# Where the norm of the differential heads is computed: ahead of the output projection, or among the products of its first two strips

## The reference

```python
def odd_mixer(h, w_qkv, w_out, lam_q1, lam_k1, lam_q2, lam_k2, subln, layer):
    ...
    y = differential_attention(q, k, v, lam)        # 8 heads, 1024 tokens, 128 features each
    y = rmsnorm(y, subln, SUBLN_EPS) * (1.0 - lam_init)   # over the 128 features of one head
    y = y.transpose(0, 2, 1, 3).reshape(B, T, N_HEADS_C * 2 * HEAD_DIM)
    return y.astype(h.dtype) @ w_out

def differential_attention(q, k, v, lam):
    ...
        p = jax.nn.softmax(s, axis=-1)
        a = p[:, :, 0] - lam * p[:, :, 1]
        return jnp.einsum('bhqk,bhkd->bhqd', a, v)
```

## Time and profile before

| | |
|---|---|
| median of 3 runs | 2777.64 us (2775.39 to 2777.65) |
| profiled execution, its own time | 2779.66 us |
| its span, first to last instruction | 2777.9 us |
| PE busy | 2682.9 us, 97% |
| DVE, ACT busy | 1773.7 us, 64%; 1114.9 us, 40% |
| chain that ended last | PE 87%, DVE 4%, ACT 4%, issue 3% |

### The profile page before, as it was taken

One profiled execution on the slowest core, in us unless ns is written; L12 is line 12 of the kernel. 1 busy time (PEld: TensorE's weight loads), 2 busy tenths in 40 slices (PEclk: granted clock), 3 DMA queues, 4 the chain that ended last, 5 costly groups with the idle time before them and its releaser, 6 DMA issues.

```text
span 2777.9 us, 37690 instructions
## 1 busy us (share of the span) xinstructions
PE 2682.9 (97%) x13632; PEld 2185.7 (79%) x13632; DVE 1773.7 (64%) x2905; ACT 1114.9 (40%) x1986; POOL 139.9 (5%) x142
## 2 busy tenths in 40 slices
PE   8999999879999999999999999999899999999998
PEld 6787777668788888888777778888787888888886
DVE  4555655554666666666667777776456667666665
ACT  4555545433432223223445445545234222322333
POOL 0000022310000000000010000000000000000001
PEclk9999999979999999999999999999999999999999
DMA  3122233441111111111211111112211111111112
GB/s 118 52 57 80 53 96 110 135 113 61 42 50 57 54 45 53 49 57 46 95 63 45 45 48 51 46 45 69 80 57 42 57 54 46 53 49 57 46 50 76
DMA packets 106220, 173.73 MB, mean 63 GB/s; under 512 B 33376, under 2 KB 42976, under 8 KB 104032
## 3 DMA queue, kind: packets, MB, share of 16 engines
q1 hardware_dynamic: 95136, 162.28, 19.1%
q10 hardware_dynamic: 10944, 9.57, 1.3%
HBM read 151.74 MB, written 20.08 MB: 62 GB/s over the span
## 4 chain that ended last, share of the span: by engine, by line
PE 87%; DVE 4%; ACT 4%; issue 3%; DMA 1%; POOL 1%; SPq 1%; ACTq 0%; POOLq 0%; DVEq 0%
PE PS L1877 18%; PE PS L1879 18%; PE PS L1878 18%; PE PS L1958 15%; PE PS L2091 4%; PE PS L2030 4%; PE PS L2053 3%; ACT EC L849 1%; PE PS L2068 1%; PE PS L2046 1%; PE PS L2015 1%; PE PS L1971 1%; PE PS L2072 1%; DVE HL L1565 1%; PE PS L1884 1%
## 5 line engine op out<-in xcount | busy, mean ns | idle before, releaser
L1958 PE MATMUL PS<-HH,WS 128*128 128x512 f32 x1536 | 527.7, 406 | 14.9 <-DVE WS L1278 11.4
L1958 PEld LDWEIGHTS PS<-HH,WS 128*128 128x128 f32 x1536 | 289.8, 190 | 74.0 <-DVE WS L1278 11.4
L1077 ACT ACTIVATE WS<-WR 128x512 fp32r<-128x512 f32 x254 | 159.3, 629 | 459.8 <-PE PS L1879 318.6
L1958 PE MATMUL PS<-HL,WS 128*128 128x512 f32 x768 | 304.0, 396 | 0.0
L1676 DVE TENSOR_TENSOR X<-PS,X 128x512 f32<-128x512 f32 x352 | 232.7, 685 | 80.6 <-PE PS L1879 78.6
L1877 PE MATMUL PS<-AH,WS 128*128 128x512 f32 x704 | 280.2, 398 | 3.1 <-issue 1.8
L1879 PE MATMUL PS<-AH,WS 128*128 128x512 f32 x704 | 278.9, 396 | 0.0
L1878 PE MATMUL PS<-AL,WS 128*128 128x512 f32 x704 | 278.5, 396 | 0.0
L1877 PE MATMUL PS<-TH,WS 128*128 128x512 f32 x640 | 251.6, 393 | 1.1 <-DVE WS L1618 1.1
L1879 PE MATMUL PS<-TH,WS 128*128 128x512 f32 x640 | 249.9, 391 | 0.0
L1878 PE MATMUL PS<-TL,WS 128*128 128x512 f32 x640 | 248.8, 389 | 0.0
(11 more groups left out here) (221 smaller groups left out, 4656.0 us busy)
## 6 DMA issues: line engine op xcount, KB each, us to landing
WR<-wstrips SPq DMA_DIRECT2D x304, 256.0 KB, 2.7
DR<-wdown SPq DMA_DIRECT2D x88, 256.0 KB, 2.6
X<-x SPq DMA_DIRECT2D x8, 1024.0 KB, 8.2
BIASC<-ali_c SPq DMA_DIRECT2D x8, 960.0 KB, 6.9
Y<-y_scratch SPq DMA_DIRECT2D x14, 512.0 KB, 8.5
BIAS<-tab_b SPq DMA_DIRECT2D x4, 1536.0 KB, 8.1
BIAS<-ali_a SPq DMA_DIRECT2D x4, 1152.0 KB, 7.9
ya_scratch<-YS ACTq DMA_DIRECT2D x32, 128.0 KB, 2.4
```

What stands on the lines that cost most here:

```text
L1077: e.activation(WS[:, slot, 0, :], src, ACT.Copy).then_inc(S["w_hi"], 1)
L1958: last = e.matmul(ps, wt, xt, start=g == 0, stop=g == 23)
```

## The change

The tiles EC0 and EC1 get two buffers each, taken in turn by blocks, and the wait before the exponential is loosened by one block. In the last pair the squares of the heads come earlier (`SQUARED_AT`), and the second strip's weights are rounded at n = 3. The mean of heads 0 to 6 stands in DVE's list at n = 6; root, reciprocal and a new way of spreading stand ahead of `hi(15, 7)` and `lo(15, 7)`: PE turns RT into rows (64 rows of 128), ACT and DVE split these into a high half (RH rows 0 to 63) and a low half (rows 64 to 127), and `y_spread` picks the two rows of a token block and head by a column of PICK that is 1 in both, broadcast as the weights, with RH as the moving operand: eight f32r matmuls of 128 columns. Two heads are spread before `pv(15, 7)` and one after it. The first two strips of the projection are then multiplied side by side in four banks, head by head, with the remaining spreads, the sums of head 7 and its old f32 `spread` among them. The third strip's weights are rounded in two single halves, and the loop over the remaining strips starts at the third.

```diff
     place[0] = stage
-    EC0 = sb("EC0", [128, T])
-    EC1 = sb("EC1", [128, T])
+    EC0 = sb("EC0", [128, 2, T])
+    EC1 = sb("EC1", [128, 2, T])
+    RH = sb("RH", [128, 128], f32r)
+    PICK = sb("PICK", [128, 64], f32r)
...
-    def e_tile(kind, m):
-        return (EC1 if m else EC0) if kind == "C" else (E1 if m else E0)
+    def e_tile(kind, m, n):
+        return (EC1 if m else EC0)[:, n % 2, :] if kind == "C" else (E1 if m else E0)
...
-        if P % 8 == 7:
+        if P == 7:
             return {1: (3, 0, 5)}
+        if P == 15:
+            return {1: (3, 0, 5), 3: (4, 1, 6)}
...
     Y_AT = {2: [0], 3: [1], 4: [2, 3], 5: [4, 5], 6: [6]}
+    SQUARED_AT = {2: [0, 1], 3: [2], 4: [3, 4], 5: [5, 6]}
...
+    SPREAD_BANK = [0, 2] + [T_BANK] * 6
...
-            turned = t_count(P, n, m if kind != "C" else 0, kind) - (2 if kind != "C" else 1)
+            turned = t_count(P, n, m if kind != "C" else 0, kind) - 2
...
+                if not after:
+                    y_root(0, KC - 1)
+                    e.wait_ge(S["rt_turned"], 1)
+                    e.activation(RH[0:64, :], PS[0:64, FILL_BANK, 128:256], ACT.Copy).then_inc(S["rt_high"], 1)
                 hi(P, n, 0, "C")
...
-                    for i in Y_AT.get(n, []):
+                    for i in SQUARED_AT.get(n, []):
                         y_square(i)
+            y_high(1, 0)
+            y_high(1, 1)
             y_keep(15, NQ - 1)
+            y_square(KC - 1)
...
         def out_projection(o):
+            N = 2 * o + 1
+            def w_half(w, slot, x):
+                e.wait_ge(S[f"raw_full{x}"], raws_strip(w, o))
+                e.activation(WS[:, 2 * slot + x, 0, :], WR[:, x, :], ACT.Copy).then_inc(S["w_hi"], 1)
             if o == 0:
+                e.wait_ge(S["fill_done"], 48 * (o + 1))
             else:
-
-                y_root(0, KC - 1)
-                for k in range(5):
+                y_high(1, 2)
+                y_high(1, 3)
+                y_root(KC - 1, KC)
+                y_high(1, 4)
+                e.wait_ge(S["op_half"], 1)
+                w_half(W_OUT[1] + 2, 0, 0)
+                for k in range(5, KC):
                     y_high(1, k)
-                y_square(KC - 1)
-                y_high(1, 5)
-                y_root(KC - 1, KC)
-                y_high(1, 6)
-                y_high(1, 7)
-            N = 2 * o + 1
-            e.wait_ge(S["fill_done"], 48 * (o + 1))
-            with e.Fori(0, KC // 2) as i:
+                e.wait_ge(S["op_done"], 1 + 16 + 2)
+                w_half(W_OUT[1] + 2, 0, 1)
+                for j in range(2):
+                    e.wait_ge(S["op_free"], 16 + 2 * j + 2 + 4)
+                    prep_chunk(N, j, j)
+            with e.Fori(o, KC // 2) as i:
...
-            e.scalar_tensor_tensor(out=EC0[:, :], in0=EC1[:, :], scalar=ST[:, n % 2, 6:7], in1=EC0[:, :],
+            e0, e1 = e_tile("C", 0, n), e_tile("C", 1, n)
+            e.scalar_tensor_tensor(out=e0, in0=e1, scalar=ST[:, n % 2, 6:7], in1=e0,
+        def y_mean(a, b):
+
+            rt = RT[:, a:b, :].rearrange("p k t -> p (k t)")
+            e.wait_ge(S["yssq_done"], b)
+            e.scalar_tensor_tensor(out=rt, in0=PS[:, FILL_BANK, NQ * a:NQ * b], scalar=1.0 / 128,
...
+        def y_reciprocal(a, b):
+            e.wait_ge(S["ysqrt_done"], 1 if a == 0 else 2)
+            e.reciprocal(rt, rt).then_inc(S["yrec_done"], 1)
+        def y_norm(k):
+            e.wait_ge(S["yspread_done"], k + 1)
+            e.scalar_tensor_tensor(out=Y[:, k, :], in0=Y[:, k, :], scalar=SUBG[:, 1:2],
+                                   in1=banks(SPREAD_BANK[k], 2), op0=ALU.mult,
+                                   op1=ALU.mult).then_inc(S["ynorm_done"], 1)
...
+                if not after:
+                    y_reciprocal(0, KC - 1)
+                    e.wait_ge(S["rt_high"], 1)
+                    e.tensor_tensor(RH[64:128, :], PS[0:64, FILL_BANK, 128:256], f(RH[0:64, :]),
+                                    ALU.subtract).then_inc(S["rt_low"], 1)
                 lo(P, n, 0, "C")
...
+                if P == 15 and n == NQ - 2:
+                    flat = "p k t -> p (k t)"
+                    e.tensor_tensor(PICK[:, :], IDENT[:, 0:64], IDENT[:, 64:128], ALU.add).then_inc(S["pick_ready"], 1)
+                    e.memset(RT[:, KC - 1, :], 1.0).then_inc(S["pick_ready"], 1)
...
+                    e.wait_ge(S["yeps_done"], 1)
+                    y_mean(0, KC - 1)
...
+            def w_half(w, slot, x):
+                e.wait_ge(S["w_hi"], 2 * w + x + 1)
+                e.tensor_tensor(WS[:, 2 * slot + x, 1, :], WR[:, x, :], f(WS[:, 2 * slot + x, 0, :]),
+                                ALU.subtract).then_inc(S["w_lo"], 1)
+
...
-                for k in range(KC + 1):
...
-                    if k:
-                        y_low(1, k - 1, k - 1)
+                y_norm(0)
+                for k in range(1, KC - 1):
+                    y_norm(k)
+                    y_low(1, k - 1, k - 1)
+                    if k == 3:
+                        y_mean(KC - 1, KC)
+                    if k == 4:
+                        y_reciprocal(KC - 1, KC)
+                w_half(W_OUT[1] + 2, 0, 0)
+                y_norm(KC - 1)
+                for k in range(KC - 2, KC):
+                    y_low(1, k, k)
...
+            def op_add(j, h, b):
+                e.wait_ge(S["op_done"], 1 + 16 * o + 2 * j + h + 1)
+                xs = X[:, j, 512 * h:512 * h + 512]
+                e.tensor_tensor(xs, PS[:, 2 * b + h, :], xs, ALU.add).then_inc(S["op_free"], 1)
+
+            if o == 1:
+                for h in range(2):
+                    op_add(0, h, 0)
+                w_half(W_OUT[1] + 2, 0, 1)
+                for h in range(2):
+                    op_add(1, h, 1)
+                for j in range(2):
+                    prep_chunk(N, j, j)
+            with e.Fori(o, KC // 2) as i:
...
+        def y_spread(k):
+
+            if k >= 2:
+                e.wait_ge(S["ynorm_done"], k)
+            for n in range(NQ):
+                last = e.matmul(PS[:, SPREAD_BANK[k] + n // 4, 128 * (n % 4):128 * (n % 4) + 128],
+                                PICK[:, NQ * k + n:NQ * k + n + 1].to_broadcast([128, 128]), RH[:, :],
+                                start=True, stop=True)
+            last.then_inc(S["yspread_done"], 1)
...
-                    for i in Y_AT.get(n - 1, []):
+                    for i in SQUARED_AT.get(n - 1, []):
                         y_sums(i)
+            e.wait_ge(S["yrec_done"], 1)
+            e.wait_ge(S["pick_ready"], 2)
+            e.transpose(PS[0:64, FILL_BANK, 128:256], RT[:, :, :].rearrange("p k t -> p (k t)"),
+                        IDENT[:, :]).then_inc(S["rt_turned"], 1)
+            e.wait_ge(S["rt_low"], 1)
+            for k in range(2):
+                y_spread(k)
             pv(15, NQ - 1, 0)
+            y_spread(2)
...
         def out_projection(o):
             if o == 1:
-
-                e.wait_ge(S["yrec_done"], 1)
+                for j in range(2):
+                    e.wait_ge(S["w_lo"], 2 * (W_OUT[1] + j) + 2)
                 for k in range(KC):
-                    if k == KC - 1:
-                        y_sums(k)
+                    e.wait_ge(S["ylo_done"], 8 + k + 1)
+                    for j in range(2):
+                        for h in range(2):
+                            if k == 0:
+                                e.wait_ge(S["op_free"], 16 + 2 * j + h + 1)
+                                e.wait_ge(S["ynorm_done"], j + 1)
+                            last = three(PS[:, 2 * j + h, :], w_tile(2 * j + k // 4, 0, k % 4),
+                                         w_tile(2 * j + k // 4, 1, k % 4), HH[:, k, 512 * h:512 * h + 512],
+                                         HL[:, k, 512 * h:512 * h + 512], k == 0, k == KC - 1)
+                            if k == 3 and (j, h) == (0, 1):
+                                last.then_inc(S["op_half"], 1)
+                            if k == KC - 1:
+                                last.then_inc(S["op_done"], 1)
+                    if k < 4:
+                        y_spread(k + 3)
+                    if k == 0:
+                        y_sums(KC - 1)
+                    if k == 4:
                         e.wait_ge(S["yrec_done"], 2)
-                    if k >= 2:
-                        e.wait_ge(S["ynorm_done"], k - 1)
-                    spread(RT[:, k, :], 2 * (k % 2), "yspread_done")
-                e.wait_ge(S["ynorm_done"], KC)
-            with e.Fori(0, KC // 2) as i:
+                        e.wait_ge(S["ynorm_done"], KC - 1)
+                        spread(RT[:, KC - 1, :], T_BANK, "yspread_done")
+            with e.Fori(o, KC // 2) as i:
```

(23 more changed lines are left out.)

23 lines of the change are left out of this document (3 added, 20 removed).

## The result

The changed kernel takes **2761.37 us** in the median of 5 runs (2758.22 to 2765.32), the kernel before, run beside it, 2777.65 (2775.39 to 2779.69). The ratio is 0.9937 [0.9925, 0.9949]: 16.3 us faster by the medians, 17.5 by the ratio.

A forecast was written before the change was run, and what follows sets the result against it. It took DVE and the hand-overs to bound the norm stage before the projection, and PE the rest; moving the third strip's start from 2000.1 to 1982.8 saves 17.3 us, giving 2760.3 from the median, range 2755.5 to 2767.5.

The forecast's parts named there:

- Buffers, 0: Exponentials in the attention: the loosened wait is already met because hi stands ahead and waits for the same transposes; 0 us.
- Strip 3, 17.3 us sooner: Output projection: the third strip's first product starts at 1982.8 instead of 2000.1, which is the whole gain.
- Sums ready at 1942.3: Last pair: all seven heads' sums are ready by 1942.3, with 0.8 us of delay taken from the earlier squares.
- Rows ready at 1944.6: Norm's head: mean, root, reciprocal, turn under 0.3 us, copy 0.3 and low half to 0.3 end at 1944.6.
- The table load, hidden: ACT before the root: the load runs between block 7's exponentials and the mean, costing 0; 1.3 us if not hidden.
- Spreads 0 and 1, 3.1 us; product by v, 3.7; spread 2, 1.2: PE after the rows: two spreads at low clock, product between the clocks, one more spread; first strip product at 1952.6.
- The two strips, 30.2 us: First two strips: products 21.8, spreads 3.8, head 7's sums 1.9, its f32 spread 2.05, switches 0.6; DVE keeps up.
- The cover of the weights: Third and fourth strips: weights are rounded before they are wanted, costing 0; 1 to 2 us if that cover failed.
- Low clock reaches into the products: Rival, chance 0.15: two heads' products in the first strips run at low clock, 5.4 us more, 2765.7 us.
- Clock full at once: Rival, chance 0.12: everything from 1944.6 runs at 2.4 GHz, the third strip starts at 1978.8, 2756.3 us.
- the dear f32r matmul: Rival, chance 0.05: in the spreads a 128-column f32r matmul costs as much as f32, 7.8 us more, 2768.1 us.
- The clock doesn't come back: Rival, chance 0.03: PE stays at 1.2 GHz through the two-strip stage, 6.4 us slower than before, 2784.0 us.

The follow-up runs named there:

- e1: The changed kernel with single buffers for EC0 and EC1 and the old wait before the exponential; 2760.95 us.
- e2: The kernel before with only the two buffers for EC0 and EC1 and the loosened wait added; 2778.30 us against 2778.19 for before.
- e10: The changed kernel unedited, run again for a second profile; 2760.47 us, ratio to before 0.9933.
- e4: The changed kernel with all spreads and norms ahead of the products, spreads 2 to 7 sharing one pair of banks; 2771.78 us.
- e12: e9 with head 7's square, sums, mean, root and reciprocal back at their old places; 2767.82 us, ratio to before 0.9958.
- e8: e4 with three pairs of banks, so a spread waits for the norm two before it; 2765.07 us.
- e9: e8 with f32 spreads in place of the f32r rows; 2764.61 us.

## Why the prediction was right

It said 2760.3, and 2761.37 and 2760.47 were measured. Point by point, its times less 2.65 us for the profile after:

- **Buffers, 0.** Right; e1 and e2 show it.
- **Strip 3, 17.3 us sooner.** Against the one profile of before it was 19.1 in the first profile of the changed kernel and 15.5 in the second, so the sum lies between them. That the median came out within 1 us, where single runs spread over 7, is partly luck.
- **Sums ready at 1942.3.** They ended at 1938.85, which is 1941.5 on the clock of before. The scores of block 4, forecast 0.8 us late behind one more square, weren't late: head 1's sums filled the wait of 1.21 us and the scores at 1911.95 waited for nothing. In other executions a rest is left (0.65 us in e10). Off by 0.8 to the good.
- **Rows ready at 1944.6.** 1941.14 + 2.65 = 1943.8: the same 0.8; the turn took 0.44, over its bound of 0.3; copy and low half, 0.28 and 0.29, were as bounded.
- **The table load, hidden.** Right. ACT's timeline:

```profile
1935.81 1.28 ACT L955 ACT_TABLE_LOAD   x1
1939.20 0.25 ACT L955 ACTIVATE RT<-RT 128x56 f32<-128x56 f32 x1 [2.11 <-DVE RT L1479]
```

  The load runs 3.4 us ahead of the root, and the root waits for DVE's mean. The Trainium skill, "ScalarE: Activation LUTs", section "What ACT_TABLE_LOAD costs", adds a drain of about 1380 ns to the load. No run here shows it: load and root were 1.30 apart when nothing stood between them, and here it would be hidden too.
- **Spreads 0 and 1, 3.1 us; product by v, 3.7; spread 2, 1.2.** Measured 3.48 (1.74 a spread at clock 0.50), 3.79, and 0.84, since the clock was back by then: 8.11 against 8.0, three errors that cancel. In e10 the product took 4.81 and in e1 5.23, so "the middle" between the clocks was a fair guess for one execution and low for the others. First product at 1949.25 + 2.65 = 1951.9 against 1952.6.
- **The two strips, 30.2 us.** 29.13, and 30.75 and 30.77 in the other two. Products 96 x 0.227 = 21.8; f32r spreads 4 x 0.84 = 3.4 (forecast 3.8 at 0.94 each); sums 1.75 (1.9); the f32 spread 1.70 (2.05: that row's own length was taken; here the record is 1.95 long and the next matmul starts 1.70 after it began); switches 0.5 (0.6). No matmul of the stage waited for DVE, ACT or the weights.
- **The cover of the weights.** Third strip's second half: rounded at 1977.88, wanted after 1981. Fourth strip's: DVE's timeline has them 6 us into strip 3, wanted at 10.9.

```profile
1984.35 1.28 DVE L1300 TENSOR_TENSOR WS<-WR,WS 128x512 fp32r<-128x512 f32 x2
```

- **The rivals.** "Low clock reaches into the products" had 0.15 and a price of 5.4 us for two heads. It came true in two of three profiled executions, at one third of the price: one head's products, 1.6 us. Here the prediction treated as either-or what varies between executions of one kernel; the first profile, 3 us better than the other two, would have hidden this. "Clock full at once" was priced for strip 3 at 1978.8; the best execution reached 1981.0. The rivals of the dear f32r matmul (0.105 us each, not the f32 price) and of helping buffers fell. "The clock doesn't come back" did not happen laid: 1.00 through the stage in the first profile, and in e10 full again after head 1 (0.94 over the stage). It did happen in e4, where PE stood still for 1.4 us in every head: 0.57 to 0.66. The Trainium skill, "TensorE: Matmul & The Clock Gate", section "HAM oscillation — how this bites in real kernels", says that bursts with waits between them can fall back to half rate; e4 agrees. But in e10 the clock was low over head 1's products (0.62 from 1956 to 1960.5) though PE had waited for nothing in the stage, so waits are not the only thing that goes with a low clock here.
- **What the sum didn't say.** It took the gain as one piece. The runs divide it: 11.9 us by the first product, or 11.7 [7.8, 15.6] by the ratio of e12, come without head 7's early chain, rows or laying: 9.8 of them are the earlier start of the norm (sums, root, load and first spreads under the attention), and 2.1 are the wait of the first product for the norm of head 7, which is gone; the prediction's sum holds this without naming it. Head 7's chain adds 0.5 to 3; f32r rows 0 to 1.2 by themselves and 1.2 to 4.7 with laying; laying, with the rows in both kernels, 2 to 5.5. The last three are near what one comparison can tell: their waits are shown in the traces, their sizes are not. No run divides the 9.8 into sums, root, load and spreads.

## What to carry to other kernels

A stage in which one engine waits for another in turns is shortened first by starting its head earlier, under work that is there anyway; that gave more than half of the gain (9.8 of the 15.5 to 19.1 us at strip 3). Cheaper instructions on an engine that waits gave little that could be told from nothing (0 to 1.2 us), so an instruction's price is best changed together with its place. Profile a kernel more than once before a detail of 2 us is read from it.

## What the hardware showed that was not expected

- **Shorter matmuls, lower clock, same time.** The stage with f32r spreads had a clock of 0.73 and the same stage with f32 spreads, each of twice the length, 1.00 (e8, e9), and the kernels took the same time within 0.5 us. That the length of the matmuls did this is not shown. In e8 the low clock lay in part in the product by v (4.31 us; 2.95 in e9) and in the last two spreads, one of which came after a wait:

```profile
1959.80 1.97 PE L2162 MATMUL PS<-RH,PICK 128*128 128x128 f32 x8 [1.25 <-DVE Y L1492]
1961.57 3.72 PE L1954 MATMUL PS<-IDENT,RT 128*128 128x128 f32 x16
```

  Between them, from 1952.7 to 1959.8, four of its f32r spreads ran with 0.90. In the changed kernel the first two f32r spreads ran at 0.50 throughout, after PE had waited 0.27 and 0.68 us.
- **Sums of one column before a drop.** Where PE waited for nothing, the scores after one head's sums took 1.65 us, after two heads' sums in a row 2.19 (e12) to 2.93. In the changed kernel's second profile:

```profile
1924.79 3.63 PE L1947 MATMUL PS<-ONES,YQ 128*128 128x1 f32 x32
1928.35 2.63 PE L2093 MATMUL PS<-KS,QS 64*128 64x512 f32 x12
```

  and in this execution and e1's head 1's products behind head 7's sums had the low clock in the same way; in the first profile they did not. PE counts as busy all the while. Whether sums laid apart, one head at a time, would keep the clock up was not tried.
- **Between 1 and 128 columns the price is per matmul, not per column.** Two columns in f32r took 0.11 us a matmul, the same as 128 columns (0.105); an f32 one of one column, with two records, took 0.22 (1.75 a head), one of 128 columns 0.21 (1.70 a spread).
